# One step of a hybrid decoder layer on eight cores: idle matmuls in the head's waits, and squares, staging, the decode projection and the first tables rearranged

## The chip, the cores and the metric

The kernel runs on the 8 cores of one Trainium2 chip. Each core takes one of the 8 prompt sequences and 16 of the 128 decode rows, so the cores run the same program on different data and exchange nothing. The metric is the device time in microseconds of the slowest core. Each core has a matrix engine (TensorE, PE in the profile; its weight loads are PEld), VectorE (DVE), ScalarE (ACT), GpSimd (POOL) and the queue engine SyncE (SP). The traces show the clock that TensorE is granted as a share of full speed; the two levels are 1.2 and 2.4 GHz.

## The reference

```python
def layer_inputs(h, norm_w, w_in, pos):          # D_MODEL = 1024, w_in 1024 x 6144
    hn = rms_norm(h, norm_w)
    u, gp, q, k, v, gr = split(hn @ w_in, 6)      # 1024 columns each
    q = rotary(split_heads(q), pos)               # 8 heads of 128
    k = rotary(split_heads(k), pos) * HEAD_DIM ** -0.5
...
# prompt: 16 meta tokens, then 2048 tokens in chunks of 128
scores = (q @ k.T) * dmask                        # gamma_h ** (i - j), j <= i
out    = scores @ v + (q * gamma ** (i + 1)) @ S
S      = gamma ** L * S + (k * gamma ** (L - 1 - i)).T @ v
# pooling branch: trailing means over 2, 4, 8, 16 rows of u, minus u, a 256 x 256 map per group
# decode: the same layer for one token per row, from a given state S and 15 given rows of u
y = rms_norm(h + concat(pool_o * silu(gp), rms(ret_o) * silu(gr)) @ w_out, final_norm_w)
```

Outputs are y for prompt and decode rows, both states S, and the last 15 rows of u for both.

## The kernel before, in words

The rows of a core are cut into 17 tiles. Tile 0 has 48 rows: the 16 decode rows and, from row 32, the 16 meta tokens. Tiles 1 to 16 have 128 prompt rows each. The weights w_in come as twelve blocks of 512 columns (blocks 0 and 1 are u, 2 and 3 the pool gate, 4 and 5 q, 6 and 7 k, 8 and 9 v, 10 and 11 the retention gate) and are cast to bf16 by the loads on GpSimd's queue; w_out comes as four such loads.

**Tiles 0 to 4 are the head.** While weights arrive, the kernel projects block by block: the list `WORD` (10, 11, 6, 7, 8, 9, 4, 5, 2, 3, 0, 1) is the order of the loads, and each block is applied to tiles 1, 2, 0, 3, 4 (`order0`) as soon as it is there. The x rows of tiles 1 to 3 are staged in parts of w_out's memory, which the weights fill only later; the same memory holds gates, k, v and the rotary's scratch buffers of these tiles.

**From tile 5 on** tile t+1 is projected, tile t goes through attention and pooling, and its output projection closes it. The 32 decode steps (`s_step`, four rows of one head's state each) are spread over tiles 5 to 15, and the decode rows' output projection, `outp(0)`, stands at the end.

**What sets the order.** The program lists tasks with engine, buffers read and written, an assumed cost and, for transfers, a size. `Prog.schedule` is a planner: it starts from these costs, gives each task a rank (the longest chain behind it), and hands every engine at each moment the ready task of highest rank among those that can start within `SLACK` of the first. PSUM's eight banks are given out by it as well. `wire` models the two groups of transfers, SP's and GpSimd's. The result is one list per engine, which the engine executes in order; between engines, semaphores wait. Transfers with `queue="w"` go out from GpSimd in the order in which they are listed.

**Names in the profile.** `A1` (L524) squares a tile's rows on ScalarE with an accumulated sum (L527), `rstd` (L506) turns the sum into a factor by a step on DVE (L508) and a power on GpSimd (L511), and DVE scales the rows (L536, from tile 5 on L532). `A2` (L556) transposes the scaled rows: for tiles 0 to 4 by TensorE through the identity (L546) with an eviction by DVE (L568), from tile 5 on by a transposing transfer `dtr` on SP (L553). The transposed tiles are `hnT`: tiles from 5 on take turns in the two halves of `hnTs`, and tiles 1 and 2 hold the same halves in the head, so tile 5 takes over the half of tile 2, and tile 6 that of tile 1. `hbufs` are the buffers of the scaled rows, `hn` for tile 1 and every tile from 5 on, `ry`, `kd`, `W`, `sgp` for tiles 2, 0, 3, 4.

`pj_mm` (its matmuls L592) is a projection of 8 matmuls with 512 columns; `gp_mm` (L609) makes gates the transposed way, 32 matmuls. `rotary` (L620) lets ScalarE evacuate a projection with a factor into a scratch buffer `Fa` (L630), writes the sine products into the projection's own PSUM bank (L643), multiplies `Fa` by the cosines (L647) and adds both into `qd` or `kd` (L649). `nextF` hands out the scratch buffers in turn: five in the head, one while u and gates of the head are projected, two later. `p_u(0)` evacuates tile 0's u twice, as f32 into a scratch buffer for a store and as bf16 into `kdM` (both through L617). `att`'s scores are L731, its outputs L755 and L757, its state L714; `pool` is L826, L828 and L845. A decode step multiplies on GpSimd (L961, into `scr`), makes an outer product on TensorE (L967), and updates the state on DVE (L969). `outp` is L904.

The head's loads are listed near the end of `build_program`: x of tile 1, the constants in one transfer (`pack`: norm weights, decays, identity, mask, band), x of the decode rows and the meta rows on SP; x of tile 2, blocks, the tables of sines and cosines (`load_cs`) and more x on GpSimd.

Of the kernel before, what the change touches and what calls it, by code (L numbers as in the profile page):

```python
# [36 lines left out]
class Prog:  # L37
# [17 lines left out]

    def op(self, eng, fn, reads=(), writes=(), sem=None, cost=0.2, size=0, bias=0.0, queue=None, pad=0.0):
        t = Task(eng, fn, reads, writes, sem, cost, size, bias)
        t.pad = pad
# [57 lines left out]
    def schedule(self):  # L116
# [18 lines left out]
        free = {e: 0.0 for e in ENGS}  # L135
        wire = {"sp": 0.0, "pool": 0.0}
        done = set()
# [15 lines left out]

        while len(done) < len(tasks):
            pick = None
            for e in ENGS:
                if not ready[e]:
                    continue
                cand = []
                for t in ready[e]:  # L160
                    s = max(est[t], free[e])
                    if t.takes is not None:
                        if not need[t] <= done:
                            continue
                        ba = bank_at(t)
                        if ba is None:
                            continue
                        s = max(s, ba[0])
                    cand.append((s, t))
                if not cand:  # L170
                    continue
                lo = min(c[0] for c in cand)
                s, t = max((c for c in cand if c[0] <= lo + SLACK[e]), key=lambda c: (c[1].rank, -c[1].i))
                if pick is None or s < pick[0]:
                    pick = (s, t)
# [8 lines left out]
            if t.size:  # L184
# [130 lines left out]
def build_program():  # L315
# [110 lines left out]
    F0h = [Buf(F0_t[:, 0:512], ["f0a"]), Buf(F0_t[:, 512:1024], ["f0b"])]  # L426
    Fsets = ([F0h[0], wof(12), wof(13), wof(14), wof(15)], [F0h[0], F0h[1]], [F0h[0]])
    Fmode, fr = [0], [0]
# [64 lines left out]
    def load_w_out(b):  # L493
        dma("pool", w_out_bf[:, b * 4:(b + 1) * 4, :].rearrange("p a b -> p (a b)"), w_out[b], [], ["wo%d%s" % (i, z) for i in range(4 * b, 4 * b + 4) for z in ("", "b")], 1 << 21, queue="w")

# [28 lines left out]
    def A1(t, xb, hb):  # L524
        T = tT(t)
        c = t % 4
        P.op("act", lambda e: e.activation(out=hb.ap[:T, :], in_=xb.ap[:T, :], func=AF.Square,  # L527
                                           accum_out=ss_x[:T, c:c + 1]), reads=xb.k + (["ss_x1"] if t == 2 else []),
             writes=hb.k + ["ss_x%d" % c], cost=c_act(1, D, acc=1))
        rstd(ss_x, rs_x, c, 1, 0, T, 1.0 / D, "ss_x%d" % c, "rs_x%d" % c, None, () if t else hnT[1].k[:1])  # L530
        if t > NG:
            P.op("dve", lambda e: e.scalar_tensor_tensor(out=hb.ap, in0=xb.ap, scalar=rs_x[:, c:c + 1], in1=normw_b[:, :],  # L532
                                                         op0=ALU.mult, op1=ALU.mult),
                 reads=xb.k + ["rs_x%d" % c, "normw_b"], writes=hb.k, cost=c_dve(1, D, ptr=1))
            return
# [20 lines left out]
    def A2(t, hb):  # L556
# [8 lines left out]
        def ev(e):  # L565
# [4 lines left out]
            return r  # L570
        P.op("dve", ev, reads=[b, "normw"], writes=d.k[:1] if n < 8 else d.k, cost=c_dve(n, T))
        if n < 8:
# [47 lines left out]
    def rotary(t, which, hh):  # L620
        T = tT(t)
        b = pj_mm(t, (2 if which == "q" else 3) * D + hh * 512)
        Fa = nextF()
        dslot = (0 if t else 2) if which == "q" else (1 if t else 3)
# [229 lines left out]
    def outp(t):  # L854
# [420 lines left out]
```

How the kernel before makes its waits and increments, by code:

```python
        def run(e, name):  # L263
            for item in self.streams[name]:
                if item[0] == "wait":
                    e.wait_ge(self.sems[item[1]], item[2])
                else:
                    _, fn, semkey, inc = item
                    fn(e).then_inc(self.sems[semkey], inc)
```

## Time and profile before

| | |
|---|---|
| median of 3 runs | 598.63 us (596.15 to 598.93) |
| profiled execution, its own time | 599.85 us |
| its span on the slowest core (6) | 598.3 us |
| spans of the cores | 589.3 to 598.3 us |
| TensorE busy | 561.6 us, 94% |
| VectorE busy | 389.7 us, 65% |
| ScalarE busy | 264.7 us, 44% |
| GpSimd busy | 110.4 us, 18% |
| moved by DMA | 79.05 MB, 132 GB/s in the mean |

All of the page is of core 6. Its span runs from the first to the last instruction; the execution's own time has 1.55 us around it. A busy share is a mean over the span: that TensorE is busy for 94% says that little of the span is left in which it waits, and the views of waits, of the granted clock by window and of the chain say where that is.

### The profile page before, as it was taken

The numbers are of one execution on the slowest core, as the hardware profiler recorded it, in microseconds if no ns is written. First come the engines' busy times: TensorE is split into PE (matmuls) and PEld (weight loads), VectorE is DVE, ScalarE is ACT, GpSimd is POOL, SyncE is SP. The second block draws the span as 40 slices with busy tenths as digits, with TensorE's granted clock in tenths as the row PEclk, the third lists the DMA queues.
The fourth block names the chain that finished last, engine by engine and source line by source line (L and its number), as shares of the span: only waits on it lengthen the run. The fifth ranks groups of instructions, "written<-read, shape, count | busy, mean of one in ns | idle before, by whom it ended". The sixth has DMA issues, their size and how long they took to land.

```text
span 598.3 us, 13978 instructions; the slowest of 8 cores (589.3 to 598.3 us)
## 1 busy us (share of the span) xinstructions
PE 561.6 (94%) x4540; PEld 317.7 (53%) x4540; DVE 389.7 (65%) x1010; ACT 264.7 (44%) x822; POOL 110.4 (18%) x133
## 2 busy tenths in 40 slices
PE   2799998988999998999999999999999999999994
PEld 1244455674545544565564646546464646556672
DVE  3358645657865856668557676868577683954665
ACT  3245454743532632543434545454453544544332
POOL 4330001120200112111112222140322220221010
PEclk9799998997999999999999999999999999999898
DMA  8999996597444624523356764567664662627203
GB/s 166 208 172 211 168 189 146 104 119 138 89 98 103 147 89 109 160 76 90 107 143 163 160 154 134 130 191 142 181 126 138 139 161 95 143 91 153 41 3 110
DMA packets 76066, 79.05 MB, mean 132 GB/s; under 512 B 55566, under 2 KB 58270, under 8 KB 74060
## 3 DMA queue, kind: packets, MB, share of 16 engines
q1 hardware_dynamic: 71836, 56.63, 37.7%
q0 software_dynamic: 4016, 21.28, 20.7%
q8 instruction: 38, 0.62, 0.5%
q14 instruction: 32, 0.26, 0.2%
q10 hardware_dynamic: 144, 0.26, 0.1%
HBM read 64.86 MB, written 18.41 MB: 139 GB/s over the span
## 4 chain that ended last, share of the span: by engine, by line
PE 83%; DMA 7%; DVE 4%; issue 3%; ACT 2%; POOL 1%; SPq 0%; DVEq 0%; POOLq 0%; ACTq 0%
PE pp L592 44%; PE pp L904 18%; PE pp L609 8%; DMA w_in_bf<-w_in 2%; PE pp L845 2%; DMA pbp<-F 2%; PE pp L826 2%; DMA hnTs<-hn 2%; PE pp L967 2%; PE pp L714 1%; PE pp L755 1%; PE pp L757 1%; PE pp L731 1%; PE pp L546 1%; DMA xr<-x 1%
## 5 line engine op out<-in xcount | busy, mean ns | idle before, releaser
L592 PE MATMUL pp<-w_in_bf,hnTs 128*128 128x512 bf16 x1120 | 261.6, 385 | 1.9 <-DMA w_in_bf<-w_in 1.1
L592 PEld LDWEIGHTS pp<-w_in_bf,hnTs 128*128 128x128 bf16 x1120 | 106.0, 99 | 124.0 <-issue 14.3
L904 PE MATMUL pp<-w_out_bf,yT 128*128 128x512 bf16 (+1 forms) x464 | 100.5, 372 | 0.8 <-PE pp L904 0.2
L511 POOL TENSOR_TENSOR sm<-sm,nh 128x4 f32<-128x4 f32 (+2 forms) x49 | 44.5, 908 | 262.1 <-DVE sm L508 258.2
L630 ACT ACTIVATE F<-pp,pack 128x128 f32<-128x128 f32 (+1 forms) x208 | 59.2, 370 | 49.1 <-PE pp L592 33.9
L904 PEld LDWEIGHTS pp<-w_out_bf,yT 128*128 128x128 bf16 x464 | 44.3, 98 | 52.0 <-issue 3.4
L961 POOL TENSOR_TENSOR scr<-vM,pack 16x512 bf16<-16x512 bf16 x32 | 36.3, 1136 | 116.4 <-PE pp L967 108.1
L609 PE MATMUL pp<-hnTs,w_in_bf 128*128 128x128 bf16 x896 | 53.1, 219 | 0.0
L911 ACT ACTIVATE pp<-xr 128x512 f32<-128x512 f32 x30 | 18.0, 601 | 78.8 <-DVE xr L909 64.0
L609 PEld LDWEIGHTS pp<-hnTs,w_in_bf 128*128 128x128 bf16 x896 | 51.1, 98 | 2.1 <-issue 0.2
L793 DVE SCALAR_TENSOR_TENSOR ry<-pp,sm,G 128x128 bf16<-128x128 f32 x104 | 29.2, 343 | 19.6 <-POOL sm L511 19.5
L592 PE MATMUL pp<-w_in_bf,xr 128*128 128x512 bf16 (+1 forms) x144 | 36.2, 400 | 2.0 <-DVE xr L568 2.0
L783 ACT ACTIVATE ry<-pp 128x128 bf16<-128x128 f32 x128 | 33.6, 290 | 9.4 <-PE pp L757 9.4
L647 DVE TENSOR_TENSOR F<-F,cs 128x512 f32<-128x512 f32 x51 | 35.0, 695 | 3.6
L909 DVE TENSOR_TENSOR xr<-xr,pp 128x512 f32<-128x512 f32 x30 | 20.6, 686 | 25.0 <-PE pp L904 24.6
L643 DVE SCALAR_TENSOR_TENSOR pp<-F,cs 128x256 f32<-128x256 f32 x51 | 22.6, 443 | 15.9 <-ACT F L630 15.5
L740 DVE SCALAR_TENSOR_TENSOR W<-pp,pack 128x128 bf16<-128x128 f32 x128 | 27.3, 279 | 6.6 <-PE pp L731 6.4
L617 ACT ACTIVATE G<-pp 128x512 bf16<-128x512 f32 x26 | 15.5, 597 | 35.9 <-PE pp L592 30.3
L769 DVE SCALAR_TENSOR_TENSOR S_f<-S_f,pp 128x128 f32<-128x128 f32 x128 | 27.4, 279 | 3.6 <-PE pp L714 3.6
L969 DVE SCALAR_TENSOR_TENSOR scr<-scr,pp 128x512 f32<-128x512 f32 x32 | 21.7, 682 | 11.3 <-PE pp L967 11.1
L617 ACT ACTIVATE us<-pp 128x512 bf16<-128x512 f32 x32 | 19.0, 599 | 21.3 <-PE pp L592 19.4
L783 ACT ACTIVATION_READ_ACCUMULATOR ry<-pp 128x1 f32 x128 | 28.2, 221 | 0.0
(180 smaller groups left out, 723.8 us busy)
## 6 DMA issues: line engine op xcount, KB each, us to landing
w_in_bf<-w_in POOLq DMA_DIRECT2D x11, 1024.0 KB, 35.6
scr<-S_in SPq DMA_DIRECT2D x32, 256.0 KB, 3.4
Ss<-scr SPq DMA_DIRECT2D x32, 256.0 KB, 3.6
xr<-x SPq DMA_DIRECT2D x15, 512.0 KB, 4.4
y<-xr SPq DMA_DIRECT2D x15, 512.0 KB, 2.9
xA<-x SPq DMA_DIRECT2D x12, 512.0 KB, 4.0
w_out_bf<-w_out POOLq DMA_DIRECT2D x4, 1024.0 KB, 11.3
w_out_bf<-x POOLq DMA_DIRECT2D x2, 512.0 KB, 11.0
```

Of the source, the lines that this page charges most:

```text
L511: P.op("pool", lambda e: e.tensor_tensor(out=rs[r0:r1, c0:c0 + n], in0=rs[r0:r1, c0:c0 + n], in1=nh[r0:r1, 0:n], op=ALU.pow), reads=[rsk, ...
L592: r = e.matmul(bk(b)[:T, :], lhsT=h.ap[:, kc * T:(kc + 1) * T], rhs=w_in_bf[:, blk, kc, :], start=(kc == 0), stop=(kc == 7))
L609: r = e.matmul(bk(b)[:, i * w:(i + 1) * w], lhsT=w_in_bf[:, blk0 + fc // 4, kc, fc % 4 * 128:(fc % 4 + 1) * 128], rhs=h.ap[:, kc * T:kc * ...
L617: P.op("act", lambda e: e.activation(out=dst() if callable(dst) else dst, in_=src(), func=func), reads=sk, writes=dk, cost=c_act(1, n))
L630: r = e.activation(out=Fa.ap[:T, i * 128:(i + 1) * 128], in_=bk(b)[:T, i * 128:(i + 1) * 128], func=AF.Copy, scale=dec[:T, dslot * 8 + h:d ...
L647: P.op("dve", lambda e: e.tensor_tensor(out=f0, in0=f0, in1=cosb, op=ALU.mult), reads=Fa.k + [b] + cs.k, writes=Fa.k, cost=c_dve(1, 512))
L740: r = e.scalar_tensor_tensor(out=W0[:, h * 128:(h + 1) * 128], in0=bk(b)[:, i * 128:(i + 1) * 128], scalar=float(GAM[h] ** -128.0), in1=ma ...
L769: r = e.scalar_tensor_tensor(out=S_f32[:, h * 128:(h + 1) * 128], in0=S_f32[:, h * 128:(h + 1) * 128], scalar=float(GAM[h] ** 128.0), in1= ...
L783: r = e.activation(out=ry_t[:, h * 128:(h + 1) * 128], in_=bk(b)[:, i * 128:(i + 1) * 128], func=AF.Square, accum_out=ss_r[:, h:h + 1])
L793: r = e.scalar_tensor_tensor(out=ry_t[:, h * 128:(h + 1) * 128], in0=bk(b)[:, i * 128:(i + 1) * 128], scalar=rs_r[:, h:h + 1], in1=gb.ap[: ...
L904: r = e.matmul(bk(b)[:T, 0:w], lhsT=yap[:, kc * 128:kc * 128 + T], rhs=w_out_bf[:, kc, sl], start=(kc == 0), stop=(kc == 15))
L961: P.op("pool", lambda e: e.tensor_tensor(out=Rh.ap[0:NS, :].rearrange("p (s v) -> p s v", s=4), in0=vM_t[0:NS, h * 128:(h + 1) * 128].unsq ...
```

## The change

It has seven edits. The lines of the changed kernel are 6 to 16 higher than those of before: L546 becomes L554, L592 L600, L609 L617, L617 L625, L527 L535, L630 L642, L731 L743, L755 and L757 L767 and L769, L961 L973, L967 L979.

- **Idle matmuls.** After tile 1 of the head, 240 tasks are listed that multiply the identity by itself into a bank that nobody reads. They may start once tile 1's first transposed columns are evicted (`go`). A task with `fill` is taken by the planner only where its engine would otherwise have nothing ready within 0.1 of plan time, and only at plan times below `fill`; 142 of the 240 come into the order (L1091), the others are left out.
- **Squares.** From tile 5 on, the square's unused output goes into the buffer of the tile's own transposed rows instead of `hn`. In the head the first step of tile 2's statistics, as tile 0's before, now stands behind tile 1's eviction.
- **Rotary.** A scratch buffer comes with a second one for the sine products, or with None, and then the PSUM bank is used as before. The head has three such sets instead of five.
- **Tile 0's u** is evacuated through `F0`'s first half and through `hn`.
- **Decode projection.** The 128 matmuls of its transposed product are eight tasks of 16 instead of one.
- **Staging.** The first transfer of `pack` on SP brings columns 0 to 111 only; mask and band follow on GpSimd's queue behind tile 2's statistics. The tables of tiles 1, 0 and 2 are loaded behind x of tile 4.
- **Planner.** In its model GpSimd's transfers start at 5.0 at the earliest, and w_out's loads get a pad of 2.0.

```diff
-        wire = {"sp": 0.0, "pool": 0.0}
+        wire = {"sp": 0.0, "pool": 5.0}
...
-                    cand.append((s, t))
+                    if t.fill is None or s < t.fill:
+                        cand.append((s, t))
...
+                work = [c for c in cand if c[1].fill is None]
+                if work and min(c[0] for c in work) <= lo + 0.1:
+                    cand = work
...
-    Fsets = ([F0h[0], wof(12), wof(13), wof(14), wof(15)], [F0h[0], F0h[1]], [F0h[0]])
+    hnf = Buf(hn_t[:, :].bitcast(F32), ["hn"])
+    Fsets = ([(F0h[0], None), (wof(12), wof(13)), (wof(14), wof(15))], [(F0h[0], None), (F0h[1], None)], [(F0h[0], hnf)])
...
+        junk = hb if t <= NG else hnT[t]
-        rstd(ss_x, rs_x, c, 1, 0, T, 1.0 / D, "ss_x%d" % c, "rs_x%d" % c, None, () if t else hnT[1].k[:1])
+        rstd(ss_x, rs_x, c, 1, 0, T, 1.0 / D, "ss_x%d" % c, "rs_x%d" % c, None, hnT[1].k[:1] if t in (0, 2) else ())
...
-        Fa = nextF()
+        Fa, Fb = nextF()
+        fk = Fb.k if Fb else [b]
...
-        P.op("dve", rot, reads=Fa.k + cs.k, writes=[b], cost=c_dve(2, 256))
+        P.op("dve", rot, reads=Fa.k + cs.k, writes=fk, cost=c_dve(2, 256))
...
-        P.op("dve", lambda e: e.tensor_tensor(out=dst, in0=Fa.ap[:T, :], in1=bk(b)[:T, :], op=ALU.add),
-             reads=Fa.k + [b], writes=dk, cost=c_dve(1, 512))
+        P.op("dve", lambda e: e.tensor_tensor(out=dst, in0=Fa.ap[:T, :], in1=fb()[:T, :], op=ALU.add),
+             reads=Fa.k + fk, writes=dk, cost=c_dve(1, 512))
...
-                Fa = nextF()
+                Fa = (F0h[0], hnf)[hh] if t == 0 else nextF()[0]
...
-            P.op("pe", mmT, reads=["yTs0", "yTs1"] + WOK, writes=[b], cost=c_pe(128, NS))
+                P.op("pe", mmT, reads=["yTs0", "yTs1"] + WOK + ([b] if dc else []), writes=[b], cost=c_pe(16, NS))
...
-    dma("sp", pack[:], c_pack[:, :], [], ["ident", "mask", "band", "dec", "normw", "retwc"], 1 << 18, queue="i")
+    dma("sp", pack[:, 0:112], c_pack[:, 0:112], [], ["ident", "dec", "normw", "retwc"], 1 << 16, queue="i")
...
-    load_cs(1, "w")
-    load_cs(0, "w")
...
-            load_cs(2, "w", ["rs_x2"])
+            dma("pool", pack[:, 112:496], c_pack[:, 112:496], ["rs_x2"], ["mask", "band"], 1 << 18, queue="w")
...
+            for c in (1, 0, 2):
+                load_cs(c, "w")
...
+        for j in range(240 if t == 1 else 0):
+            b = Bank()
+            P.op("pe", lambda e, b=b: e.matmul(bk(b)[:, 0:128], lhsT=ident[:, :], rhs=ident[:, :], start=True, stop=True),
+                 reads=["ident", "go"], writes=[b], cost=0.056, fill=32.0)
```

TensorE's order in the head, before, from its first matmul to block 11's first sixteen (the last row). The scaled rows hn, ry, kd and W are those of tiles 1, 2, 0 and 3; hnTs and xr hold transposed tiles, L592 is a projection and L609 a gate of tile 0:

```order
L546 MATMUL pp<-pack,hn 128x128 x8
L546 MATMUL pp<-pack,ry 128x128 x8
L592 MATMUL pp<-w_in_bf,hnTs 128x512 x12
L546 MATMUL pp<-pack,kd 128x48 x8
L592 MATMUL pp<-w_in_bf,hnTs 128x512 x4
L609 MATMUL pp<-xr,w_in_bf 128x16 x32
L546 MATMUL pp<-pack,W 128x128 x8
L592 MATMUL pp<-w_in_bf,xr 128x512 x4
L592 MATMUL pp<-w_in_bf,hnTs 128x512 x16
```

The same stretch after, from behind tile 2's transposes (ry), ahead of which 29 idle matmuls stand; the next row is block 11's `L600` x16:

```order
L1091 MATMUL pp<-pack 128x128 x3
L554 MATMUL pp<-pack,kd 128x48 x8
L600 MATMUL pp<-w_in_bf,hnTs 128x512 x4
L1091 MATMUL pp<-pack 128x128 x15
L600 MATMUL pp<-w_in_bf,hnTs 128x512 x4
L1091 MATMUL pp<-pack 128x128 x9
L600 MATMUL pp<-w_in_bf,hnTs 128x512 x8
L617 MATMUL pp<-xr,w_in_bf 128x16 x32
L1091 MATMUL pp<-pack 128x128 x44
L554 MATMUL pp<-pack,W 128x128 x8
L1091 MATMUL pp<-pack 128x128 x42
L600 MATMUL pp<-w_in_bf,xr 128x512 x4
```

Idle matmuls (L1091) now stand in six places, the last two, 44 and 42, around tile 3's transposes. Tile 1's sixteen projections on blocks that are there stood as twelve and four around tile 0's transposes; now all stand behind these, as four, four and eight. On ScalarE tile 0's square (kd) has moved ahead of tile 2's (ry).

TensorE around the transposes of tile 1's rotated q (qd), before; hnTs x8 in the third row is tile 1's last q projection:

```order
L592 MATMUL pp<-w_in_bf,xr 128x512 x16
L592 MATMUL pp<-w_in_bf,F 128x512 x8
L592 MATMUL pp<-w_in_bf,hnTs 128x512 x8
L592 MATMUL pp<-w_in_bf,F 128x512 x12
L546 MATMUL pp<-pack,qd 128x128 x8
L592 MATMUL pp<-w_in_bf,xr 48x512 x16
L731 MATMUL pp<-qT,kT 128x128 x8
```

The same place after; tile 1's last q projection is the first row:

```order
L600 MATMUL pp<-w_in_bf,hnTs 128x512 x8
L600 MATMUL pp<-w_in_bf,xr 48x512 x8
L600 MATMUL pp<-w_in_bf,F 128x512 x16
L554 MATMUL pp<-pack,qd 128x128 x8
L617 MATMUL pp<-xr,w_in_bf 128x16 x32
L600 MATMUL pp<-w_in_bf,hnTs 128x512 x8
L743 MATMUL pp<-qT,kT 128x128 x8
```

Between the last q projection and the transposes stood twelve matmuls of tile 4 (F); now eight of tile 0 and sixteen of tile 4 stand there.

ScalarE where tile 5's transposed rows have been sent for and tile 6's square (the first row, L527) begins, before; kdM and F are tile 0's u:

```order
L527 ACTIVATE hn,sm<-xA 128x1024
L630 ACTIVATE F<-pp,pack 128x128 x4
L617 ACTIVATE scr<-pp 128x1024
L617 ACTIVATE kdM<-pp 48x512
L617 ACTIVATE F<-pp 16x512
L617 ACTIVATE kdM<-pp 48x512
L617 ACTIVATE us<-pp 128x512
```

ScalarE after, at tile 5's square (the fourth row), which writes hnTs, and GpSimd's queue of the same stretch below it, with w_out's loads (L485):

```order
L625 ACTIVATE w_out_bf<-pp 128x512 x3
L625 ACTIVATE us<-pp 128x512 x2
L625 ACTIVATE w_out_bf<-pp 128x512 x2
L535 ACTIVATE hnTs,sm<-xA 128x1024
L625 ACTIVATE w_out_bf<-pp 128x512
L625 ACTIVATE sgps<-pp 128x64
L625 ACTIVATE scr<-pp 128x1024
```

```order
L518 TENSOR_TENSOR sm<-sm,nh 128x4 x2
L485 DMA w_out_bf<-w_out 128x4096
L518 TENSOR_TENSOR sm<-sm,nh 128x4 x2
L518 TENSOR_TENSOR sm<-sm,nh 128x1
L485 DMA w_out_bf<-w_out 128x4096 x2
L518 TENSOR_TENSOR sm<-sm,nh 128x4 x2
```

The square has left hn, and tile 0's u (kdM) has moved ahead of this stretch. Two loads of w_out now follow each other in one row on GpSimd's queue; before, each of the four stood alone, with statistics (L511) between them. From tile 2's last gate projection to tile 5's first projection, TensorE's order after has these in a row: 32 matmuls of a gate, 16 of pooling, 8 pairs of pooling, 8 of the state, 32 of 16 columns, 16 of pooling, 8 transposes, 8 scores, 64 of gates, 16 projections and 8 pairs of attention. DVE's order has six evacuations of pooling between the first step of tile 5's statistics and its scaling. The first two decode outer products (L979), which followed each other, now have eight projections between them.

## Rows read from the trace of the kernel before

**Rows 1.** Cores: span from first to last instruction, mean granted clock of TensorE.
```profile
core 1: 596.5 us, clock 0.985
...
core 6: 598.3 us, clock 0.978
```

**Rows 2.** Windows, core 6: length, engines' busy time (PE first), PEclk, DMA, GB/s.
```profile
26.00:30.00 4.00, 4.00 (x12) 1.41 (x11) 0.78 (x2) 1.15 (x2) 0.55 (x1) 0.54 1.01 175
150.00:598.00 448.00, 435.53 (x3483) 245.78 (x3481) 303.24 (x766) 194.79 (x625) 84.36 (x89) 0.99 0.49 122
...
94.00:98.00 4.00, 3.85 (x14) 0.57 0.68 168
```

**Rows 3.** Waits, TensorE of core 6: total us, times, longest us.
```profile
PE pp L826 <- ACT kdM L617: 4.0, 1, 4.0
...
PE pp L967 <- POOL scr L961: 3.0, 2, 2.0
...
PE pp L546 <- issue: 1.9, 1, 1.9
PE pp L546 <- DVE qd L649: 1.4, 1, 1.4
```

**Rows 4.** Timeline, TensorE in the head: start, duration, work, [idle before <- releaser].
```profile
8.57 1.01 PE L546 MATMUL pp<-pack,hn 128*128 128x128 bf16 x8 [8.57 <-DVE hn L536]
...
26.40 5.26 PE L592 MATMUL pp<-w_in_bf,hnTs 128*128 128x512 bf16 x16
```

**Rows 5.** Chain that ended last: start, duration, engine, tile and line.
```profile
33.38 0.45 PE pp L546 x8
...
34.69 0.79 PE pp L609 x32
...
60.12 3.45 PE pp L592 x16
...
79.89 0.70 DVE qd L649
...
138.79 3.54 PE pp L592 x8
```

**Rows 6.** DMA issues from 7.9 to 8.7 us: KB each, median us to landing.
```profile
w_in_bf<-w_in POOLq DMA_DIRECT2D x1, 1024.0 KB, 17.3
```

**Rows 7.** Timeline of the head, the other engines.
```profile
8.00 0.59 POOL L478 DMA_DIRECT2D w_in_bf<-w_in  x1 [0.54 <-POOL sm L511]
...
9.52 1.06 ACT L527 ACTIVATE ry<-w_out_bf 128x1024 bf16<-128x1024 f32 x1 [3.05 <-DMA w_out_bf<-x]
...
10.48 0.19 ACT L527 ACTIVATION_READ_ACCUMULATOR ry<-w_out_bf 128x1 f32 x1
...
11.67 1.06 ACT L527 ACTIVATE kd<-xA 48x1024 bf16<-48x1024 f32 x1 [1.00 <-DMA xA<-meta]
...
11.75 0.75 DVE L536 TENSOR_SCALAR ry<-w_out_bf,sm 128x1024 bf16<-128x1024 f32 x1 [0.83 <-POOL sm L511]
...
13.78 1.63 DVE L568 TENSOR_SCALAR hnTs<-pp,pack 128x128 bf16<-128x128 bf16 x8
...
19.06 1.29 DVE L568 TENSOR_SCALAR xr<-pp,pack 128x48 bf16<-128x48 bf16 x8 [3.01 <-PE pp L546]
```

**Rows 8.** Timeline, TensorE before the first rotated q transposes.
```profile
80.83 0.61 PE L546 MATMUL pp<-pack,qd 128*128 128x128 bf16 x8 [1.44 <-DVE qd L649]
```

**Rows 9.** Timeline around tile 5's transposing transfer.
```profile
120.55 0.59 POOL L478 DMA_DIRECT2D w_out_bf<-w_out  x1 [2.02 <-DVE ry L793]
...
133.40 1.06 ACT L527 ACTIVATE hn<-xA 128x1024 bf16<-128x1024 f32 x1 [4.88 <-DMA hnTs<-hn]
```

**Rows 10.** DMA issues: one from 123 to 125 us, then over the whole run.
```profile
hnTs<-hn SPq DMA_TRANSPOSE x1, 9.4
...
hnTs<-hn SPq DMA_TRANSPOSE x12, 3.5
```

**Rows 11.** The page's groups: busy us, mean ns of one, idle before.
```profile
L617 ACT ACTIVATE us<-pp 128x512 bf16<-128x512 f32 x32 | 19.0, 599 | 21.3 <-PE pp L592 19.4
```

More of the change, by code:

```diff
@@ L54, in ps, with op @@
         return self.stack.enter_context(self.nc.psum_tensor(name, list(shape), dt))
-    def op(self, eng, fn, reads=(), writes=(), sem=None, cost=0.2, size=0, bias=0.0, queue=None, pad=0.0):
+    def op(self, eng, fn, reads=(), writes=(), sem=None, cost=0.2, size=0, bias=0.0, queue=None, pad=0.0, fill=None):
         t = Task(eng, fn, reads, writes, sem, cost, size, bias)
-        t.pad = pad
+        t.pad, t.fill = pad, fill
         if queue is not None:
@@ L152, in bank_at @@
             return best
-        while len(done) < len(tasks):
+        total, real = len([t for t in tasks if t.fill is None]), 0
+        while real < total:
             pick = None
@@ L193, in schedule @@
             done.add(t)
+            real += t.fill is None
             order.append(t)
@@ L493, in load_w_out @@
     def load_w_out(b):
-        dma("pool", w_out_bf[:, b * 4:(b + 1) * 4, :].rearrange("p a b -> p (a b)"), w_out[b], [], ["wo%d%s" % (i, z) for i in range(4 * b, 4 * b + 4) for z in ("", "b")], 1 << 21, queue="w")
+        dma("pool", w_out_bf[:, b * 4:(b + 1) * 4, :].rearrange("p a b -> p (a b)"), w_out[b], [], ["wo%d%s" % (i, z) for i in range(4 * b, 4 * b + 4) for z in ("", "b")], 1 << 21, queue="w", pad=2.0)
     def fold_w_out():
@@ L526, in A1 @@
         c = t % 4
-        P.op("act", lambda e: e.activation(out=hb.ap[:T, :], in_=xb.ap[:T, :], func=AF.Square,
+        junk = hb if t <= NG else hnT[t]
+        P.op("act", lambda e: e.activation(out=junk.ap[:T, :], in_=xb.ap[:T, :], func=AF.Square,
                                            accum_out=ss_x[:T, c:c + 1]), reads=xb.k + (["ss_x1"] if t == 2 else []),
-             writes=hb.k + ["ss_x%d" % c], cost=c_act(1, D, acc=1))
-        rstd(ss_x, rs_x, c, 1, 0, T, 1.0 / D, "ss_x%d" % c, "rs_x%d" % c, None, () if t else hnT[1].k[:1])
+             writes=junk.k + ["ss_x%d" % c], cost=c_act(1, D, acc=1))
+        rstd(ss_x, rs_x, c, 1, 0, T, 1.0 / D, "ss_x%d" % c, "rs_x%d" % c, None, hnT[1].k[:1] if t in (0, 2) else ())
         if t > NG:
@@ L570, in ev @@
             return r
-        P.op("dve", ev, reads=[b, "normw"], writes=d.k[:1] if n < 8 else d.k, cost=c_dve(n, T))
+        P.op("dve", ev, reads=[b, "normw"], writes=d.k[:1] + ["go"] if n < 8 else d.k, cost=c_dve(n, T))
         if n < 8:
@@ L622, in rotary, with fb @@
         b = pj_mm(t, (2 if which == "q" else 3) * D + hh * 512)
-        Fa = nextF()
+        Fa, Fb = nextF()
+        fk = Fb.k if Fb else [b]
+        def fb():
+            return Fb.ap if Fb else bk(b)
         dslot = (0 if t else 2) if which == "q" else (1 if t else 3)
@@ L641, in rot @@
         def rot(e):
-            f1 = bk(b)[:T, :].rearrange("p (h two j) -> p h two j", h=4, two=2)
+            f1 = fb()[:T, :].rearrange("p (h two j) -> p h two j", h=4, two=2)
             e.scalar_tensor_tensor(out=f1[:, :, 0, :], in0=f0[:, :, 1, :], scalar=-1.0, in1=sinb,
@@ L645, in rot @@
             return e.tensor_tensor(out=f1[:, :, 1, :], in0=f0[:, :, 0, :], in1=sinb, op=ALU.mult)
-        P.op("dve", rot, reads=Fa.k + cs.k, writes=[b], cost=c_dve(2, 256))
+        P.op("dve", rot, reads=Fa.k + cs.k, writes=fk, cost=c_dve(2, 256))
         P.op("dve", lambda e: e.tensor_tensor(out=f0, in0=f0, in1=cosb, op=ALU.mult),
-             reads=Fa.k + [b] + cs.k, writes=Fa.k, cost=c_dve(1, 512))
-        P.op("dve", lambda e: e.tensor_tensor(out=dst, in0=Fa.ap[:T, :], in1=bk(b)[:T, :], op=ALU.add),
-             reads=Fa.k + [b], writes=dk, cost=c_dve(1, 512))
+             reads=Fa.k + fk + cs.k, writes=Fa.k, cost=c_dve(1, 512))
+        P.op("dve", lambda e: e.tensor_tensor(out=dst, in0=Fa.ap[:T, :], in1=fb()[:T, :], op=ALU.add),
+             reads=Fa.k + fk, writes=dk, cost=c_dve(1, 512))
     def p_u(t):
@@ L866, in outp, with mmT @@
             b = Bank()
-            def mmT(e, b=b):
-                r = None
-                for dc in range(8):
+            for dc in range(8):
+                def mmT(e, b=b, dc=dc):
+                    r = None
                     for kc in range(16):
@@ L873, in mmT @@
                                      rhs=yTs[:, kc * NS:(kc + 1) * NS], start=(kc == 0), stop=(kc == 15))
-                return r
-            P.op("pe", mmT, reads=["yTs0", "yTs1"] + WOK, writes=[b], cost=c_pe(128, NS))
+                    return r
+                P.op("pe", mmT, reads=["yTs0", "yTs1"] + WOK + ([b] if dc else []), writes=[b], cost=c_pe(16, NS))
             r1, r2 = sc67.ap[:, 0:128], sc67.ap[:, 128:256]
```

## The prediction

> **What bounds the kernel now.** I read the cores first, then TensorE's waits, its clock by stage, the head's timeline, and the chain where TensorE stood still. The slowest core sets the time: core 6 with 598.3 us; core 1 comes next with 596.5 [rows 1]. The profiled execution took 599.85 us, 1.55 more than its span; the median of the runs shown is 598.63, 1.2 below it.
>
> From 150 to 598 us core 6's TensorE is busy for 435.5 of 448 us at a granted clock of 0.99 [rows 2]. So this is a TensorE kernel, and what can be won lies where TensorE waits, and in the stretches behind such waits in which the clock is granted at 0.5, that is 1.2 instead of 2.4 GHz. Behind the wait for the first normalised tile, which stays, the list of its waits [rows 3] names them: 4.0 us for ScalarE's evacuation into kdM, 3.0 for GpSimd, 1.9 that end with "issue", 1.4 for the rotated q. The clock rows show low stretches at 26 to 30 and 94 to 98 us [rows 2]: the first at the end of a head full of waits, the second behind the 1.9 us stall; behind the 4.0 us wait eight matmuls took 3.54 us where sixteen take 3.45 [rows 5].
>
> **The change part by part.**
>
> Head, idle matmuls and squares. Block 11's first sixteen matmuls take 5.26 us from 26.40, until 31.66 [rows 4]; sixteen at the full clock take 3.45 [rows 5], so they lose 1.8 us to the clock. The order now puts idle matmuls into these waits: 29, 3, 15 and 9, then 44 and 42 around tile 3's transposes. At the full clock eight of that shape take 0.45 us, 0.056 each [rows 5]; at the start eight took 1.01, 0.126 each [rows 4]. The last 86 cost 4.8 us at the full clock. They stand in order ahead of block 11, whose weights land at 8.00 + 17.3 = 25.3 us [rows 6, 7], so they hide only as long as something else is late.
>
> Something is. On ScalarE tile 0's square now stands ahead of tile 2's. In the trace it starts at 11.67, having waited for the meta rows [rows 7], and 1.25 later (1.06 + 0.19) tile 2's starts, at 12.92 instead of 9.52. I follow it: square over at 14.2; 1.1 to the scaling (from 10.67, the square's end before, to 11.75) at 15.2; its 0.75, transposes 1.0, tile 2's eviction of 1.63 over at 18.6, tile 0's of 1.3 at 19.9. Then by the order: nine idle and eight real matmuls (2.2), tile 0's 32 short ones (0.8 [rows 5]), 44 idle (2.5), tile 3's transposes and eviction (0.5 + 1.8, over which the 42 idle ones run for 2.4), four real (0.9). Block 11 begins at 28.7 and its sixteen, now at the full clock, end at 32.2, against 31.66: **+0.5**. At best tile 2's chain isn't late and the sixteen start as block 11 lands: 25.3 + 3.45 = 28.75, -2.9. At worst the 86 run at 0.126 (+6.0) and the clock stays low (+1.8): +8.3. I take the chain that I followed.
>
> The smaller pack transfer, the later tables and the first eviction ahead of tile 2's statistics cost nothing: TensorE has until 25.3 for this work. If the pack's smaller part brings the meta rows sooner, that is the good side of the range.
>
> Rotary through pairs of SBUF buffers. DVE's instructions stay in number and size; the sum, L649, which reads PSUM now, takes 0.70 for 512 columns [rows 5], and with both inputs in SBUF I take the same, as nothing shorter is shown. Cost 0 (-1 to +1); a bank comes free earlier. In exchange there are three sets instead of five. In the new order 24 matmuls of 0.216 us (3.45 / 16) stand between tile 1's last q projection and the transposes of its rotated q, 5.2 us, where twelve (2.6) stood. The chain through ScalarE and DVE ended with L649 at 80.59, and the transposes began at 80.83 after 1.44 us of idling [rows 5, 8], so it outlasts twelve matmuls by 1.44 and is over well within 24. So the 1.44 us wait goes: **-1.4**. It could come back elsewhere (-1.4 to +1.4).
>
> Squares into the transposed tile's buffer. On core 6 ScalarE stood 4.88 us before tile 6's square, which writes hn, until hn's transposing transfer, issued between 123 and 125, had landed 9.4 us later; behind it stood the evacuation for which TensorE waited 4.0 us [rows 3, 9, 10]. The eight matmuls of 3.54 us behind that wait lose 1.8 to the clock (3.54 - 3.45 / 2) [rows 5]. These 5.8 us go, since the square no longer waits for hn, and tile 0's u projection now stands far earlier.
>
> What is late next is tile 5's own transfer. Its square now writes hnT of tile 5, the buffer of tile 2, so it waits for tile 2's last gate projection. From there: one evacuation 0.6 [rows 11]; the square 1.25 [rows 7]; 0.3 for DVE's first step of the statistics, a part of the 1.1 above; DVE's six evacuations of 512 columns in front of the scaling, 6 x 0.70 = 4.2, with GpSimd's step beside them; the scaling, 1,024 columns, as two of 0.70, 1.4; the transfer 9.4 if it is as slow as that one. Together 17.2 us. Between that projection and tile 5's first matmul TensorE has, by the order, 32 + 16 + 16 + 8 + 32 (16 columns) + 16 + 8 + 8 + 64 + 16 (512 columns) + 16 matmuls: 1.8 + 0.9 + 0.65 + 0.45 + 0.8 + 0.9 + 0.45 + 0.45 + 3.6 + 3.45 + 0.9 = 14.3 us at full clock rates. So it waits 2.9 us, and I add 1.7 for a low stretch behind it, as the 1.9 us stall had one (3.85 us busy at 0.57 lose 1.7) [rows 2]: 4.6 back. With 3.5 us, the median of the twelve such transfers [rows 10], there is no wait. The slow one ran beside a w_out load issued at 120.55 [rows 9]; now two w_out loads stand in POOL's queue there, so I take the 9.4. Net **-1.2** (-5.8 to +8.2, the latter with a transfer twice as slow, 9.4 more).
>
> Tile 0's u projection through F0 and hn. Its second half no longer waits for the first half's store; tile 5's scaling must wait for hn's store, which by the order is long issued. Cost 0.
>
> The stall of 1.9 us [rows 3] and the 1.7 of low clock behind it belong to no edit, and on core 1 no such stall is among the waits. Without them core 1, at 596.5, is next [rows 1]: **-1.8**.
>
> Decode steps. The first two outer products stood back to back, and the longer of the two waits for GpSimd's row, 2.0 of the 3.0 us [rows 3], stands before the second; eight 512-column matmuls now stand between. The 3.0 us go. A new order leaves gaps elsewhere; in 150 to 598 us TensorE was idle 12.5 us [rows 2], room for either sign. I let 2 come back: **-1.0** (-3 to +3).
>
> Decode projection in eight pieces. The same 128 matmuls, with seven more completions between them, now fill places between other work. TensorE was dense there, so I take 0 (-1 to +0.5).
>
> Sum: 0.5 - 1.4 - 1.2 - 1.8 - 1.0 = -4.9, so 594.95 against the execution's own 599.85, and 593.7 against the median. I forecast **594.3**, between the two, and count the rivals from there.
>
> **Rivals.**
>
> Tile 5's transfer is quick. For it: the median of twelve is 3.5 us [rows 10]; against it: the w_out loads beside it. 4.6 less: 589.7.
>
> The idle matmuls hold up real work. Each is its own step that waits for the bank's former user and reports its end, which the eight transposes in one step don't. At the cold 0.126 instead of 0.056 the 86 take 6.0 us more, and nothing hides that after 25.3: 600.3. For it: nothing in the trace shows such single steps. Against it: the eight in 0.45 [rows 5]. The Trainium skill (TensorE: Matmul & The Clock Gate, Back-to-back issue gap) speaks for part of it: a stream of weight load and matmul pairs at 128 columns sustains some 81 ns, not the isolated 56. By that the 86 take 2.2 us more, an estimate from that page; the trace disagrees for pairs within one step (eight in 0.45).
>
> The idle matmuls don't keep the clock: tile 3's wait still has a low stretch behind it. 1.8 more: 596.1.
>
> Slower: tile 5's transfer, behind the reload of x on SP and beside two w_out loads, takes twice 9.4. TensorE waits 12.3 instead of 2.9: 603.7. It makes the kernel slower by over 0.5% from about 17 us on. For it: 9.4 against 3.5 with such a load beside it. Against it: the 9.4 is the longest that I found, with POOL's queue already full of w_out.
>
> **How the numbers follow.** About 0.5%, 3 us, is what a measurement of this kernel can tell from no change: faster is below 595.6, slower above 601.6. Forecast 0.48, quick transfer 0.17, hold-up 0.15, clock not kept 0.08, slow transfer 0.12. Of the forecast's cases (591 to 598) some 70% lie below 595.6, with the quick transfer and a third of the clock case that makes 0.54 faster; most of the hold-up and the rest of the forecast give 0.31; the slow transfer and the bad tail of the hold-up 0.15. The range reaches from the quick transfer to the hold-up with a little more: 588.5 to 601.5.
>
> **What would show it.** Right: full clock from about 18 us to beyond 40; block 11's first matmul at 28 to 29 us; no TensorE wait for kdM, but one of 2 to 4 us for hnTs<-hn before tile 5's first projection, with a low stretch; no wait for scr of L961's successor; idle matmuls 56 to 65 ns apart. Wrong: block 11 begun before 27 or after 30 us, or no wait at tile 5, or one above 6 us.

## The result and the profile after

The changed kernel takes 634.38 us (median of 4 runs, 631.27 to 636.92) against 598.78 beside it: a ratio of 1.061 [1.053, 1.068]. I had forecast 594.3. In all six executions that list their cores, two or four of them take 627 to 635 us at a mean granted clock of 0.94, and the others 605 to 614. Single executions of 636 to 707 us, with cores at means down to 0.81, came with several kernels (two of 25 of before, one each of e3, e7 and e8, two each of e10 and e14); counts and ratios below leave them out, medians hold them. The cores of the profiled execution (mean clock of the span behind each):

```profile
core 0: 609.8 us, clock 0.984
core 1: 612.2 us, clock 0.982
core 2: 629.7 us, clock 0.943
core 3: 627.0 us, clock 0.945
...
core 6: 606.9 us, clock 0.988
```

So there are two losses. The undisturbed cores take 606 to 612 us where those of before took 589 to 598; the slowest of them, core 1, is 14 us above the slowest of before ([rows 1]), core 6 itself 8.6. And a pair takes 15 to 18 more than core 1. Windows of core 2 (length, TensorE's busy time and matmuls, PEclk, DMA share, GB/s):

```profile
30.00:42.00 12.00, 11.92 (x85) 1.00 1.01 170
42.00:43.00 1.00, 1.00 (x6) 0.95 1.06 180
43.00:100.00 57.00, 56.96 (x267) 0.81 0.92 170
...
200.00:205.00 5.00, 5.00 (x22) 0.87 0.67 161
205.00:600.00 395.00, 390.95 (x3055) 1.00 0.51 130
```

and the same stretch on core 6:

```profile
43.00:100.00 57.00, 56.17 (x363) 1.00 0.94 181
```

From 43 to about 203 us core 2 runs at 0.81, neither of the two levels of [rows 2]; both cores are busy nearly throughout these 57 us, and core 2 gets through 267 matmuls, core 6 through 363 (of other kinds too, so their ratio isn't that of the clocks). No row of before shows 0.81.

What the other cores lose is in two places. The head, core 6 (start, duration, engine, work):

```profile
10.85 1.06 ACT L535 ACTIVATE kd<-xA 48x1024 bf16<-48x1024 f32 x1 [4.79 <-DMA xA<-meta]
...
11.90 1.04 ACT L535 ACTIVATE ry<-w_out_bf 128x1024 bf16<-128x1024 f32 x1
...
13.94 2.99 PE L1091 MATMUL pp<-pack 128*128 128x128 bf16 x23 [2.92 <-ACT hnTs L586]
14.19 0.77 DVE L544 TENSOR_SCALAR ry<-w_out_bf,sm 128x1024 bf16<-128x1024 f32 x1 [0.78 <-POOL sm L518]
...
16.89 1.01 PE L554 MATMUL pp<-pack,ry 128*128 128x128 bf16 x8
...
18.02 1.63 DVE L576 TENSOR_SCALAR hnTs<-pp,pack 128x128 bf16<-128x128 bf16 x8 [2.17 <-PE pp L1091]
...
25.32 5.77 PE L1091 MATMUL pp<-pack 128*128 128x128 bf16 x44
...
37.62 3.62 PE L600 MATMUL pp<-w_in_bf,hnTs 128*128 128x512 bf16 x16
```

The 44 idle matmuls take 5.77 us, 0.131 each at a granted clock of 1.00, not the 0.056 of eight in one step [rows 5]. Block 11's sixteen run at the full clock, as they were meant to, but end at 41.2 instead of 31.7 us [rows 4]. The 23 idle ones do harm as well: tile 2's scaled rows are ready at 14.96, and its transposes start at 16.89, as soon as those 23 are through. From there to block 11 TensorE hardly pauses, so nearly every idle matmul behind it counts.

Tile 5, core 6, same columns (the first row ends with tile 2's last gate projection):

```profile
135.02 3.74 PE L617 MATMUL pp<-hnTs,w_in_bf 128*128 128x128 bf16 x64
...
139.35 1.05 ACT L535 ACTIVATE hnTs<-xA 128x1024 bf16<-128x1024 f32 x1
...
143.14 0.59 POOL L485 DMA_DIRECT2D w_out_bf<-w_out  x1 [1.56 <-PE pp L726]
...
145.10 1.28 DVE L540 SCALAR_TENSOR_TENSOR hn<-xA,sm,normw_b 128x1024 bf16<-128x1024 f32 x1
145.79 0.53 POOL L485 DMA_DIRECT2D w_out_bf<-w_out  x1 [2.06 <-DVE scr L863]
...
146.50 1.35 SPq L561 DMA_TRANSPOSE hnTs<-hn  x1
...
161.94 5.14 PE L600 MATMUL pp<-w_in_bf,hnTs 128*128 128x512 bf16 x16 [8.89 <-DMA hnTs<-hn]
```

TensorE waits 8.89 us for the transposing transfer and then loses 1.5 to the clock (5.14 against 3.62). The transfer's landing, among the DMA issues from 140 to 148 us (KB each, median us to landing):

```profile
w_out_bf<-w_out POOLq DMA_DIRECT2D x2, 1024.0 KB, 12.8
...
hnTs<-hn SPq DMA_TRANSPOSE x1, 15.3
```

It takes 15.3 us, where the slow one of before took 9.4 [rows 10]. The other undisturbed cores wait 8.9 to 11.1 us for it. Among TensorE's waits on core 6 (total, times, longest) those of [rows 3] for kdM and "issue" are gone or small, and the one for GpSimd's row has shrunk:

```profile
PE pp L600 <- DMA hnTs<-hn: 8.9, 1, 8.9
...
PE pp L979 <- POOL scr L973: 0.5, 1, 0.5
```

### The profile page after: what moved, and what is told of

The parts are those of the page before. It is cut to its first block, busy times and chain, and to the rows that moved or that the text cites. A ratio compares the mean times of both kernels' runs of the same rounds, so it can differ in the third digit from the quotient of the medians.

```text
span 629.7 us, 14417 instructions; the slowest of 8 cores (606.0 to 629.7 us)
## 1 busy us (share of the span) xinstructions
PE 596.7 (95%) x4682; PEld 339.7 (54%) x4682; DVE 388.8 (62%) x1010; ACT 263.9 (42%) x822; POOL 106.9 (17%) x134
## 4 chain that ended last, share of the span: by engine, by line
PE 92%; DMA 3%; DVE 2%; issue 1%; ACT 1%; POOL 0%; POOLq 0%; DVEq 0%; ACTq 0%; SPq 0%
PE pp L600 49%; PE pp L916 18%; PE pp L617 9%; PE pp L1091 3%; DMA hnTs<-hn 3%; PE pp L857 2%; PE pp L838 2%; PE pp L979 2%; PE pp L554 1%; PE pp L726 1%; PE pp L767 1%; PE pp L743 1%; PE pp L769 1%; DMA w_out_bf<-x 1%; PE pp L884 1%
## 5 line engine op out<-in xcount | busy, mean ns | idle before, releaser
L600 PE MATMUL pp<-w_in_bf,hnTs 128*128 128x512 bf16 x1120 | 266.7, 390 | 10.6 <-DMA hnTs<-hn 8.4
L600 PEld LDWEIGHTS pp<-w_in_bf,hnTs 128*128 128x128 bf16 x1120 | 106.8, 100 | 135.7 <-issue 40.2
L642 ACT ACTIVATE F<-pp,pack 128x128 f32<-128x128 f32 (+1 forms) x216 | 61.4, 371 | 60.9 <-PE pp L600 46.7
L617 PE MATMUL pp<-hnTs,w_in_bf 128*128 128x128 bf16 x896 | 54.3, 222 | 0.0
L973 POOL TENSOR_TENSOR scr<-vM,pack 16x512 bf16<-16x512 bf16 x32 | 35.4, 1106 | 107.3 <-PE pp L979 102.1
L617 PEld LDWEIGHTS pp<-hnTs,w_in_bf 128*128 128x128 bf16 x896 | 52.1, 99 | 2.2 <-issue 0.8
L655 DVE SCALAR_TENSOR_TENSOR pp<-F,cs 128x256 f32<-128x256 f32 x53 | 23.7, 447 | 28.7 <-ACT F L642 28.4
L600 PE MATMUL pp<-w_in_bf,xr 128*128 128x512 bf16 (+1 forms) x144 | 39.9, 433 | 0.0
L659 DVE TENSOR_TENSOR F<-F,cs 128x512 f32<-128x512 f32 x53 | 36.6, 699 | 3.9 <-DVE pp L657 0.5
L625 ACT ACTIVATE G<-pp 128x512 bf16<-128x512 f32 x26 | 15.5, 597 | 37.6 <-PE pp L600 36.2
L625 ACT ACTIVATE us<-pp 128x512 bf16<-128x512 f32 x32 | 19.1, 600 | 27.1 <-PE pp L600 24.3
L515 DVE TENSOR_SCALAR sm<-sm 128x4 f32<-128x4 f32 (+2 forms) x49 | 7.4, 157 | 35.8 <-ACT ry L795 15.7
```

The source lines that it names most:

```text
L600: r = e.matmul(bk(b)[:T, :], lhsT=h.ap[:, kc * T:(kc + 1) * T], rhs=w_in_bf[:, blk, kc, :], start=(kc == 0), stop=(kc == 7))
L617: r = e.matmul(bk(b)[:, i * w:(i + 1) * w], lhsT=w_in_bf[:, blk0 + fc // 4, kc, fc % 4 * 128:(fc % 4 + 1) * 128], rhs=h.ap[:, kc * T:kc * ...
L625: P.op("act", lambda e: e.activation(out=dst() if callable(dst) else dst, in_=src(), func=func), reads=sk, writes=dk, cost=c_act(1, n))
L642: r = e.activation(out=Fa.ap[:T, i * 128:(i + 1) * 128], in_=bk(b)[:T, i * 128:(i + 1) * 128], func=AF.Copy, scale=dec[:T, dslot * 8 + h:d ...
L973: P.op("pool", lambda e: e.tensor_tensor(out=Rh.ap[0:NS, :].rearrange("p (s v) -> p s v", s=4), in0=vM_t[0:NS, h * 128:(h + 1) * 128].unsq ...
```

## The experiments

Theory A: the idle matmuls bring the 0.81. Theory B: the denser order of the other edits does. "With 0.81" is read from the profile or, for executions that weren't profiled, from two or more cores at a mean clock of 0.93 to 0.95. The runs were made on two chips, e5 to e8 on one, e1 to e4 and e9 to e15 on the other, each beside before on its own.

**e1, no idle matmuls.** The other rows of every engine's order stay the same.

```diff
-        for j in range(240 if t == 1 else 0):
+        for j in range(0):
```

> The changed kernel without its 142 idle matmuls; every other row of every engine's order is the same. Theory A (the idle matmuls are what brings two or more cores to a granted clock of 0.81 from about 43 to 203 us): all cores at 0.97 or more over the span, no 0.81 from 50 to 150 us, spans 600 to 612 us as on the undisturbed cores now, less about 4 us because block 11 starts near 30 instead of 36 us: about 603 us. Theory B (the denser order of the other edits alone does it): still 628 to 634 us with a pair of cores at 0.94. In both the wait for tile 5's transposing transfer stays at 8 to 10 us.

606.47 us against 601.26, ratio 1.009 [1.006, 1.012]; all cores at 0.973 or more. A holds, B falls.

**e2, the idle matmuls in the kernel before** (the planner's rule, `go` and the 240 tasks, of which 85 come into the order).

> The kernel before with the idle matmuls alone (planner rule and 240 tasks). Theory A: a pair of cores at 0.81 from about 45 us on and 0.94 to 0.95 over the span, 618 to 630 us. Theory B: no core at 0.81; the idle matmuls at 0.126 us each only hold up block 11 by some 5 us: 600 to 604 us.

621.91 us, six executions of six with 0.81, against 601.26. Windows of its core 4:

```profile
35.00:36.00 1.00, 1.00 (x12) 0.81 0.91 147
36.00:195.00 159.00, 155.56 (x1104) 0.81 0.66 126
195.00:200.00 5.00, 4.97 (x35) 0.96 0.42 127
```

Here it is the four cores of one die, from 35 us, again for some 160 us. The idle matmuls alone bring it, and fewer of them than in the change: 74 stand ahead of block 11 (the last row), 11 behind it.

```profile
15.57 0.64 PE L1085 MATMUL pp<-pack 128*128 128x128 bf16 x5
...
19.49 1.48 PE L1085 MATMUL pp<-pack 128*128 128x128 bf16 x14
...
21.69 1.63 PE L1085 MATMUL pp<-pack 128*128 128x128 bf16 x13
...
23.78 5.28 PE L1085 MATMUL pp<-pack 128*128 128x128 bf16 x42
...
29.83 3.62 PE L598 MATMUL pp<-w_in_bf,hnTs 128*128 128x512 bf16 x16
```

**e3, tile 5's square in hn**, the rest as in the change.

```diff
-        junk = hb if t <= NG else hnT[t]
+        junk = hb if t <= 5 else hnT[t]
```

> The changed kernel, only tile 5's square writes hn again as before (tiles 6 to 16 as in the change). If the wait of 8 to 10 us is the lateness of that square: the transposing transfer is issued some 8 us earlier, ahead of the last two w_out loads, lands in under 10 us, TensorE's wait for hnTs goes below 2 us, every core's span is 8 to 12 us shorter (undisturbed cores 595 to 602), and the time is 620 to 626 us because the 0.81 stays. Rival (the transfers of that stretch are slow whenever they start): the transfer still takes 15 us and a wait of 5 us or more stays, 626 to 632 us.

627.44 us; four cores at 0.945 to 0.947, the other four with spans of 595.7 to 598.0 (in the change 606 to 612). The transfer is issued at 138.83 on core 0, lands 3.1 us later, and no wait for it is left.

**e4, both.**

> Both: no idle matmuls and tile 5's square in hn. If theory A and the lateness of the square are right the two add: 592 to 598 us, no faster than about 590, all cores at 0.98 or more. If B is right: 618 to 626 us.

595.14 us, ratio 0.990 [0.986, 0.993], faster than before. From e1 it differs by the square's place alone: 11.3 us. The transfer on core 6, ahead of the w_out loads:

```profile
hnTs<-hn SPq DMA_TRANSPOSE x1, 4.7
```

**e5, idle matmuls by eight**, with tile 5's square in hn.

```diff
-        for j in range(240 if t == 1 else 0):
+        for j in range(30 if t == 1 else 0):
...
+                for i in range(8):
+                    r = e.matmul(bk(b)[:, 0:128], lhsT=ident[:, :], rhs=ident[:, :], start=True, stop=True)
...
-                 reads=["ident", "go"], writes=[b], cost=0.056, fill=32.0)
+            P.op("pe", idle, reads=["ident", "go"], writes=[b], cost=0.45, fill=32.0)
```

> The changed kernel with tile 5's square in hn, and the idle matmuls in steps of eight with one completion each (160 of them). Theory C (each idle matmul as its own step costs 0.126 to 0.131 us where one inside a step costs 0.056): eight take 0.45 to 0.6 us, block 11 starts at 28 to 30 instead of 36.7 us, and spans of cores at the full clock are 587 to 591 us instead of 596 to 598. Rival (0.13 is what a 128-column matmul with its own weight load takes here, in a step or not): eight take 1.0 us, nothing moves. The clock: theory A says that a pair of cores at 0.81 stays (612 to 622 us); if the long idle stretch of single steps is needed for it, no 0.81 and 589 to 593 us.

594.26 us, ratio 0.991 [0.988, 0.994], no 0.81. TensorE on core 6:

```profile
21.91 2.84 PE L1094 MATMUL pp<-pack 128*128 128x128 bf16 x48
...
27.83 3.62 PE L600 MATMUL pp<-w_in_bf,hnTs 128*128 128x512 bf16 x16
```

0.059 us each, and block 11 begins ten microseconds earlier than in the change. Theory C holds: it is the step, not the matmul, that costs 0.131. Each step reports its end and takes a bank of its own; which of the two costs it is not separated.

**e6, zeros** in place of the identity, in single steps.

```diff
-lhsT=ident[:, :], rhs=ident[:, :]
+lhsT=yTs[:, 0:128], rhs=yTs[:, 0:128]
```

> The changed kernel with tile 5's square in hn, and the idle matmuls multiply zeros instead of the identity; the order is the same. Theory D1 (what the idle matmuls draw themselves brings the 0.81): no core at 0.81, 597 to 601 us. Theory D2 (they only keep the clock up, so that all cores enter block 11 at the full clock without a pause, and that brings it): still 0.81 on two or more cores from 35 to 45 us on, 620 to 628 us.

602.07 us, ratio 1.004 [1.002, 1.006], no 0.81 in ten executions. The time on TensorE is the same as with the identity (core 2):

```profile
25.20 5.77 PE L1092 MATMUL pp<-yTs 128*128 128x128 bf16 x44
```

D2 falls as far as chips may be compared: the same order with the identity (e3) ran on the other chip. On e6's chip single identity steps, fewer of them, brought 0.81 in four of eleven executions (e8). What stays is the hold-up, a ratio of 1.004 against e4's 0.990, some 8 us.

**e7 and e8, only the first 56, only the last 91** (`fill=17.3`; a key that tile 0's eviction writes in place of `go`).

> The changed kernel with tile 5's square in hn, and only the first 56 idle matmuls, those ahead of tile 0's gates; the wait for tile 3's transposes is empty again. Theory D2: a stretch at 0.5 stands between 24 and 32 us on most cores, no 0.81, 594 to 599 us. Theory D1, or a sum over the head: 0.81 on some cores in some executions, 615 to 622 us.

> The changed kernel with tile 5's square in hn, and only the idle matmuls behind tile 0's transposes (5 and the 86 around tile 3's). Theory D2: no stretch at 0.5 before block 11, 0.81 on two or more cores from some 5 us behind block 11's start, 618 to 628 us. If the whole head has to be filled for it: no 0.81, 596 to 600 us, the hold-up alone.

e7: 597.4 us, ratio 0.997 [0.994, 1.000], no 0.81 in nine. e8: seven executions of 598 to 601 us, four of 621 to 624. By itself that looks like a count: none of nine with 56 single steps, four of eleven with 91, all eight with 142 (e3). But e3 ran on the other chip, and there e2's 85, 74 of them ahead of block 11, brought it in six of six. So the number alone doesn't set how often it comes; chip and place are not separated.

**e9, the change again, and e10, the change with its idle matmuls by eight.**

> The changed kernel once more, to stand on one chip beside the next three. If the 0.81 belongs to the kernel: again 0.81 on two or more cores in every execution, 628 to 637 us. If it belongs to the chip that it ran on: no 0.81 here, 610 to 614 us.

> The changed kernel, only the idle matmuls in steps of eight (160); tile 5's square stays as in the change. Single steps as the cause of both the hold-up and the 0.81: no 0.81, block 11 at 28 to 30 us, the wait of 8 to 10 us for tile 5's transfer stays, 604 to 608 us. Rival (the 0.81 was the earlier chip's, or the late square's): 0.81 on a pair of cores, 622 to 630 us.

e9: three executions of 634 to 636 us, and two of 612.5 and 613.0 without 0.81, which by themselves stand at 1.020 [1.016, 1.024]; one of these was profiled, its slowest core:

```profile
core 1: 610.9 us, clock 0.983
```

So the 0.81 isn't in every execution, and without it the change is still 13 us slower. e10: 604.65 us, ratio 1.008 [1.004, 1.011], no 0.81 in six; the wait for the transfer stays (9.8 us on core 3). Grouping alone gives back 8 us of hold-up, and no 0.81 of the change's kind is left.

**e11 and e13, tile 0's square behind tile 2's**, with the idle matmuls by eight (e11) and without any (e13).

```diff
-reads=xb.k + (["ss_x1"] if t == 2 else []),
+reads=xb.k + (["ss_x1"] if t == 2 else ["ss_x2"] if t == 0 else []),
```

> Idle matmuls by eight, tile 5's square in hn, and tile 0's square behind tile 2's on ScalarE, as it stood before the change. My step that tile 2's chain is late by the meta rows' landing: tile 2's transposes 2 to 3 us earlier, block 11 at 25.5 to 27.5 us, 590 to 593 us. Rival (block 11's start is set by the idle matmuls themselves or by its weights): as with the square ahead, 593 to 596 us. In both no 0.81.

> No idle matmuls at all, tile 5's square in hn, tile 0's square behind tile 2's. If the idle matmuls by eight are worth what they were put there for (block 11's first sixteen at the full clock instead of 4.2 to 5.7 us): 593.5 to 595.5 us, 1 to 3 us above the 592.4 with them. Rival (they hold up as much as they give back): 591 to 593 us, the same.

592.39 us, ratio 0.985 [0.982, 0.988], and 592.38 us, ratio 0.986 [0.983, 0.990]: the best of all, and the same. The square's place is worth 2 to 4 us (their ratios against those of e5 and e4; for the smaller figure the intervals overlap). Tile 2's chain was late by it, but block 11 gains less than I had expected of e11: it begins 0.2 to 1.6 us earlier than on the same cores of e5, and 0.6 to 2.8 earlier in e13 than in e4. The rival on the idle matmuls holds. Block 11 on core 3, e5, e11, e4 and then e13:

```profile
28.31 3.62 PE L600 MATMUL pp<-w_in_bf,hnTs 128*128 128x512 bf16 x16
```

```profile
27.82 3.62 PE L600 MATMUL pp<-w_in_bf,hnTs 128*128 128x512 bf16 x16
```

```profile
28.25 4.52 PE L600 MATMUL pp<-w_in_bf,hnTs 128*128 128x512 bf16 x16
```

```profile
27.64 4.62 PE L600 MATMUL pp<-w_in_bf,hnTs 128*128 128x512 bf16 x16
```

By eight, the idle matmuls do give this core a microsecond of clock (3.62 against 4.62); over the eight cores nothing of it reaches the time.

**e12, by sixteen (320), and e14 with e15, single again and by two (212).**

> Tile 5's square in hn, and as many idle steps as by eight but of sixteen matmuls each (320), so that they fill the head about as long as the 142 single ones did; block 11 begins near 36 us. Theory D1 with time (what draws current without a pause for some 30 us brings the 0.81, however it is cut into steps): 0.81 on two or more cores, 615 to 630 us. Rival (single steps are needed for it): no 0.81, the hold-up alone, 598 to 603 us.

> The single idle steps with tile 5's square in hn once more, as the base for the next one on its chip. 0.81 in half or more of its executions at 622 to 628 us, the others at 597 to 601 us.

> As before it, but two idle matmuls in each step (212). Theory E (steps with one matmul and a pause of some 70 ns behind it are what brings the 0.81; steps without such a pause don't): a step of two takes 0.13 to 0.19 us, no or few executions with 0.81, 596 to 601 us. Rival (any identity matmul in short steps does it): 0.81 about as often as with single steps, 618 to 626 us.

e12: 600.21 us, ratio 1.000 [0.998, 1.002], no 0.81 in ten, although block 11 begins at 35.5 to 37.2 us: D1 with time falls. e14: seven executions of 624 to 629 us, all with 0.81, against 599.14. e15, same chip: 599.68 us, ratio 1.000 [0.998, 1.002], no 0.81 in ten. Cores of e14:

```profile
core 3: 600.0 us, clock 0.993
core 4: 620.0 us, clock 0.947
```

and TensorE of e15:

```profile
25.55 4.41 PE L1094 MATMUL pp<-pack 128*128 128x128 bf16 x66
```

A step of two takes 0.134 us, hardly more than a step of one (0.067 for each matmul), and the 0.81 is gone. Theory E fits all runs; why some executions of a kernel with single steps have no 0.81 it doesn't say, and that the pause behind each single matmul is the cause, and not something else in such steps, is argued, not shown.

## Why the prediction was wrong

**Idle matmuls.** The failed step is "eight of that shape take 0.45 us, 0.056 each", carried over from eight transposes in one step. Each idle matmul is a step that reports its end; the last 86 take 11.1 us (5.77 and 5.3), not 4.8. My bound of 0.126 for them was near it, and the rival "hold up real work" named the mechanism; I gave it 0.15. The sum also had no term for the 29, 3 and 15 further ahead: 23 of them alone held tile 2's transposes until 16.89, and the whole head is late by 8.9 us (block 11 at 37.6, not 28.7). A small slip stands in it too: the 42 behind tile 3's transposes were counted with the eviction's 1.8 us, not their own 2.4. All this cost 8 us of the time (e9's undisturbed executions against e10; 6 to 7 against e1).

**The clock.** The prediction knew two levels, and only cases in which idle matmuls raise the clock or don't. The third, 0.81 on two or four cores, had no rival. It costs 22 us (e9: 634.5 against 612.5), more than half of the 40 by which I missed; without it the change would still lie 18 above my forecast. The Trainium skill (TensorE: Matmul & The Clock Gate, Seeing it yourself) tells of a limiter that takes a die to 13/16, 0.81, once three of its cores run dense matmuls, holds it there while the load lasts, and is not set off by zeros. The level agrees with these runs, and e6's ten executions with zeros don't speak against it; the rest doesn't agree: in its profiled execution before keeps all eight cores at a mean of 0.978 or more under the same load (its lowest is core 6, [rows 1]), in the change cores 2 and 3 fall alone, and it ends after some 160 us although the load goes on.

**Tile 5's square.** The mechanism was right, the place and the wait too ("it waits 2.9 us"), its size was not: 8.9 us and 1.5 of clock. The mis-sized term is the transfer, put at 9.4 and measured at 15.3, with two w_out loads and x of tile 6 beside it. Issued ahead of those loads it took 4.7 (e4); that it is they that slow it is argued, as no run moved the loads alone. The chain up to it came out: 7.7 us from tile 2's last gate projection to the issue, where I had 7.8, and 14.3 of TensorE's work beside all of it, as I had. The rival that doubled the transfer put the wait at 12.3; the 8.9 to 11.1 of the undisturbed cores lie nearer to it than to 2.9. e4 against e1 puts it at 11.3 us.

**Right.** The kdM wait (5.8 with its clock) is gone; the wait for GpSimd went from 3.0 to 0.5; the 1.9 us stall didn't come back on the undisturbed cores; tile 2's rows were late by the meta rows (ready at 14.96, where I had followed them to 16.0), though in the change its transposes then stood behind idle matmuls. Tile 1's rotated q is no longer waited for, but a wait for a sum of the rotary came back at the end, on core 4:

```profile
516.74 3.29 PE L600 MATMUL pp<-w_in_bf,hnTs 128*128 128x512 bf16 x8 [1.68 <-DVE qd L661]
```

which with its low clock (3.29 where half of 3.62 is full speed) takes more than the 1.4. Without the idle matmuls and tile 5's square the other edits are worth 6 us (e4). That this is near the -4.9 of my sum is luck: the terms of it that e4 keeps (-1.4, -5.8, -1.8, -1.0) come to -10.0, and 4 us of them didn't come or were lost elsewhere; where, no run separates. Together: -6 + 11 + 8 make the 13 of e9's undisturbed executions, and 22 for the 0.81 the rest.

## What to carry to other kernels

Count steps, not instructions: a matmul that signals its own end took 0.131 us where one inside a step took 0.059, so work that is to fill a wait belongs in steps of several. Idle matmuls can cost more clock than they keep: look at the granted clock of all cores behind them, and first ask whether the kept clock reaches the time at all (e11 against e13: it didn't). When a buffer is swapped to end a wait, follow what the new buffer's former reader delays, and take a transfer's time from the busiest stretch that it can fall into.

## What the runs showed that I had not expected

A granted clock of 0.81 that starts some 5 us behind block 11's first matmuls (35 us in e2, 43 in the change) and lasts for about 160 us in every profile that has it; it takes a pair of cores or a whole die, and came only with single identity matmuls in a step: in 24 of 26 executions with 142 of them, six of six with e2's 85, four of eleven with e8's 91, none of nine with e7's 56; in none with zeros and none with two or more in a step. Why a denser stream of the same matmuls doesn't bring it, and why not every execution with single steps has it, stays open.
